# Moving the residual's normalization and the copies of the attention heads in the queues of VectorE and ScalarE

## The reference

```python
x = layer_norm(ALPHA * x + mixer, ln1_g, ln1_b)
q = (x @ wq); k, v = split(mem @ wkv)            # 4 heads of 256, 256 memory tokens
p = softmax(q k^T / 16); o = p v                 # per head
x = layer_norm(ALPHA * x + o @ wo, ln2_g, ln2_b)
```

## Time and profile before

| What | Value |
|---|---|
| Median of 3 runs | 884.2 us (882.92 to 884.68) |
| Profiled execution: its own time | 888.07 us |
| Its span in the trace | 886.3 us |
| Mean granted clock of TensorE | 0.975 |
| PE busy | 856.4 us (97%) |
| PE, DVE and ACT in the chain of work that ended last | 67%, 18% and 8% of the span |
| DVE busy | 666.4 us (75%) |
| ACT busy | 484.6 us (55%) |
| DMA, mean over the span | 188 GB/s |

### The profile page before, as it was taken

The page is one execution under the profiler, slowest core; times in us unless marked ns, Lnnn a source line. Parts: engine busy times, 40 slices in busy tenths (PEclk is TensorE's granted clock), DMA queues, the critical chain, the costliest instruction groups (busy, mean ns, idle before and its releaser), DMA issues.

```text
span 886.3 us, 15964 instructions
## 1 busy us (share of the span) xinstructions
PE 856.4 (97%) x6420; PEld 810.8 (91%) x6420; DVE 666.4 (75%) x1076; ACT 484.6 (55%) x730; POOL 7.7 (1%) x17
## 2 busy tenths in 40 slices
PE   8999999999979999999997999999999999999997
PEld 7889987999879999999997999899899999999885
DVE  5787787867667888888867896787797687776553
ACT  5643456556547666655456756565657454444452
POOL 0200000000000000000000000000000000000000
PEclk9999999999978999999998999999999899999999
DMA  9886658854132766567872365475566377775751
GB/s 338 242 264 197 206 188 245 248 169 133 61 118 85 227 186 181 182 199 262 276 245 85 119 180 157 142 229 171 171 214 190 97 230 227 235 222 183 173 207 48
DMA packets 139593, 166.91 MB, mean 188 GB/s; under 512 B 5520, under 2 KB 123280, under 8 KB 139520
## 3 DMA queue, kind: packets, MB, share of 16 engines
q1 hardware_dynamic: 137712, 162.82, 58.6%
q0 software_dynamic: 720, 2.02, 1.2%
q10 hardware_dynamic: 1088, 1.05, 0.3%
HBM read 164.62 MB, written 1.25 MB: 187 GB/s over the span
## 4 chain that ended last, share of the span: by engine, by line
PE 67%; DVE 18%; ACT 8%; issue 4%; DMA 2%; SPq 1%; DVEq 0%; ACTq 0%
PE ps L529 67%; DVE lor L1721 7%; DVE FA L1724 3%; ACT hir L1161 3%; DVE FA L1721 2%; DMA raw<-in_w_in 1%; DVE raw L1738 1%; DVE X L1721 1%; DVE FA L1727 1%; DMA raw<-in_ffn_w_down 1%; DVE X L1724 0%; DVE FA L2472 0%; ACT FA L1287 0%; ACT FA L1601 0%; PE ps L774 0%
## 5 line engine op out<-in xcount | busy, mean ns | idle before, releaser
L1721 DVE TENSOR_TENSOR lor<-raw,hir 128x1024 fp32r<-128x1024 f32 (+1 forms) x267 | 308.5, 1176 | 93.0 <-ACT hir L1161 90.0
L1161 ACT ACTIVATE hir<-raw 128x1024 fp32r<-128x1024 f32 (+1 forms) x257 | 258.3, 1030 | 103.6 <-PE ps L529 85.1
L529 PE MATMUL ps<-INH,hir 128*128 128x256 f32 (+2 forms) x1000 | 288.7, 289 | 1.8 <-ACT INH L1329 1.2
L529 PE MATMUL ps<-INH,lor 128*128 128x256 f32 (+2 forms) x1000 | 284.6, 285 | 2.8 <-DVE lor L1721 2.7
L529 PE MATMUL ps<-INL,hir 128*128 128x256 f32 (+2 forms) x1000 | 284.9, 285 | 0.8 <-DVE INL L1721 0.6
L529 PE MATMUL ps<-HIH,hir 128*128 128x256 f32 (+1 forms) x752 | 216.6, 288 | 0.0
L529 PE MATMUL ps<-HIH,lor 128*128 128x256 f32 (+1 forms) x752 | 213.6, 284 | 2.1 <-DVE lor L1721 2.1
L529 PE MATMUL ps<-HIL,hir 128*128 128x256 f32 (+1 forms) x752 | 212.5, 283 | 0.0
L529 PEld LDWEIGHTS ps<-INH,lor 128*128 128x128 f32 x1000 | 191.9, 192 | 5.1 <-DVE lor L1721 4.0
L529 PEld LDWEIGHTS ps<-INH,hir 128*128 128x128 f32 x1000 | 192.1, 192 | 4.7 <-issue 3.4
L529 PEld LDWEIGHTS ps<-INL,hir 128*128 128x128 f32 x1000 | 191.8, 192 | 1.7 <-DVE INL L1721 1.7
(11 more groups left out here) (284 smaller groups left out, 802.1 us busy)
## 6 DMA issues: line engine op xcount, KB each, us to landing
raw<-in_w_in SPq DMA_DIRECT2D x64, 512.0 KB, 4.5
raw<-in_mod_wT SPq DMA_DIRECT2D x48, 512.0 KB, 4.7
raw<-in_ffn_w_up SPq DMA_DIRECT2D x44, 512.0 KB, 4.0
raw<-in_w_ffn_in SPq DMA_DIRECT2D x44, 512.0 KB, 4.8
raw<-in_w_ffn_out SPq DMA_DIRECT2D x22, 512.0 KB, 4.7
raw<-in_ffn_w_down SPq DMA_DIRECT2D x20, 512.0 KB, 5.9
raw<-in_xa_wkv SPq DMA_DIRECT2D x16, 512.0 KB, 4.5
raw<-in_xa_wq SPq DMA_DIRECT2D x8, 512.0 KB, 5.1
```

Source lines behind the costliest of these rows:

```text
L529: return e.matmul(o, l, r, start=start, stop=stop, skip_group_check=True)
L1161: e.activation(hi, src, ACT.Copy).then_inc(*w_hi.up(i))
L1721: return e.tensor_tensor(o, a, b, op)
```

## The change

The normalization of the residual is moved in both queues, and the order of the last two heads against the splits. Nothing is added to or taken from what is computed. PE's and SP's own orders are unchanged.

On DVE `normed(0)` goes in front of `settle(0)` and `normed(1)` behind `settle(1)`. `normed(2)` and `normed(3)` stand right behind `shares(3)`, and `next(xo[1])` goes behind all copies and splits of heads 2 and 3. On ACT `affine(0)` stands before `settle(0)`, `affine(1)` before `expo(0)`, and `turned(2)` and `turned(3)` follow `expo(3)` directly; `next(xo[1])` stands behind `oc_put(3)`.

```diff
@@ scalar @@
             ahead.more()
             ahead.more()
-            settle(0)
-            settle(1)
...
+            affine(0)
+            settle(0)
+            settle(1)
             ahead.unit(("xq", 2), 8)
+            affine(1)
             expo(0)
             expo(1)
             settle(2)
...
             oc_put(0)
             oc_put(1)
             expo(3)
-            affine(0)
-            affine(1)
-            next(xo[1])
             turned(2)
             turned(3)
             affine(2)
             oc_put(2)
+            affine(3)
             oc_put(3)
+            next(xo[1])
             next(xo[2])
-            affine(3)
             for c in range(4):
@@ vector @@
             run(late)
+            normed(0)
             settle(0)
             settle(1)
+            normed(1)
             ahead.more()
             ahead.more()
...
             greatest(3)
             oc_put(1)
             shares(3)
-            normed(0)
-            normed(1)
-            next(xo[1])
             normed(2)
+            normed(3)
             oc_copy(2)
             oc_put(2)
             oc_copy(3)
             oc_put(3)
+            next(xo[1])
             next(xo[2])
-            normed(3)
             for c in range(4):
```

## The result

The changed kernel takes 881.86 us (median of 20 runs, 879.02 to 886.11) against 884.55 us for the kernel before, measured beside it (20 runs, 882.92 to 887.68). The ratio is 0.9972 with a 95% interval of 0.9960 to 0.9983, so it is faster by 0.28%, some 2.5 us (the medians differ by 2.7). One execution of the last kernel of the experiments took 1661.23 us, nearly twice as long as any other; it is left out of that kernel's median.

A forecast was written before the change was run, and what follows sets the result against it. PE, busy 97% of the span, was taken as the bound except in a few waits. Terms 0 + 1.1 - 1.05 - 3.1 = -3.05 us gave 881.15 us from a median of 884.2; range 878.6 to 884.6.

The forecast's parts named there:

- a half clock between 221 and 250: Sign that the prediction is wrong: PE's clock at half somewhere from 221 to 250 us, in the memory attention.
- `normed(0)` in DVE's idle time, cost 0: Before 197.80 us DVE idles 1.83 us for PE; normed(0), 1.37 us, fits into it and costs nothing.
- `normed(1)` reaches PE in full, 1.1 us: DVE has no idle time before the splits at 201.60; the delay makes PE begin near 223.0, 1.1 us late.
- Given back out of the wait for ACT's copy: PE's wait of 1.33 us before 231.25 absorbs the lateness, giving back 1.05 us, net loss 0.05.
- 3.6 us the most: PE's floor: residual 0 can't come before 240.5, so at most 3.6 us without changing the pattern.
- The tail, 3.1 us: DVE and ACT from 226 lose two normed and two affine; residual of chunk 0 at 241.0 instead of 244.07.
- Nothing late at 240.5 for the moved split: Second half of xo1 is split by 238.8, PE wants it at 240.5: 1.7 us to spare.
- Rival 2: PE's pause at 221.6 grows to about 1.35 us and its clock falls, losing 4.2 us: 885.3; chance 0.10.
- return "one step later": After a clock fall in the pause at 221.6, full clock returns a step later, making 886.5 instead of 885.3.
- two terms of 0.8 us for friction and for the clock's steps: Allowances in the bounds: 0.8 us of queue friction against the gain, about 0.8 for what clock steps add or take.
- Rival 1: Half-clock stretch still runs 254.7 to 271.8 though work comes earlier, giving back 1.5 us: 882.7; chance 0.20.
- Rival 3: PE's clock stays full through the second normalization, saving 4.5 us more: 876.6; chance 0.07.

The follow-up runs named there:

- last kernel of the experiments: The order only kernel with residual 3 and its square moved in front of the two splits; 878.45 us against 884.73 before, ratio 0.9922.
- chunk 1 late: Changed kernel with normed(1) and affine(1) put back behind the last softmax; 880.80 us against 884.71 before, ratio 0.9957.
- order only: Changed kernel with all four norms behind the last softmax, copies of heads 2 and 3 still ahead of the splits; 880.09 us against 884.71 before, ratio 0.9948.
- norms-only kernel: Changed kernel with norms of chunks 0 and 1 still early, splits and last norm back between and behind the copies; 885.47 us against 884.71 before, ratio 1.0009.
- delay-twice kernel: Changed kernel with two more norm-sized DVE instructions behind normed(1), output unchanged; 883.65 us against 884.73 before, ratio 0.9995.

## Why the prediction was right

Forecast were 881.15 us and a gain of 3.05 us; measured were 881.86 us and a ratio of 0.9972, 2.5 us. The mechanism is the forecast one, but one of the prediction's own signs of being wrong, a half clock between 221 and 250, came in the first trace. Point by point:

- *`normed(0)` in DVE's idle time, cost 0*: right. The idle time shrank from 1.83 to 0.43 us and the scores began where they had (204.62, with the whole stage 0.17 later).
- *`normed(1)` reaches PE in full, 1.1 us*: right and shown both ways. Taken back it gave 1.0 us of B (27.38 to 26.38), doubled it lengthened the pause by another 1.33.
- *Given back out of the wait for ACT's copy*: right for this kernel, from 1.33 to 0.25 us in every trace with the new order. But the wait goes as well where PE is not late (chunk 1 late, order only), so the lateness bought nothing: it is 1.0 us that the change could have kept. The prediction called 3.6 us the most that was to be had, because it took PE's lateness into its floor; the order-only kernel gained 4.0 us in B.
- *The tail, 3.1 us*: right. From head 3's product to three splits in a row to residual 0; B is 2.99 us shorter where the clock did not fall. What carries it is the order, not the early norms: the early norms alone changed nothing that the runs can tell, the order alone gained 4 us. Which part of the order carries it was not tried: in every kernel `normed(3)` moved ahead of the copies together with `next(xo[1])` behind them. The prediction had counted "two `normed` and two `affine`" less as what the tail loses, and that was not the reason. They have cover there: behind the other two norms DVE is idle for head 2 for 3.5 us, 4.48 in the trace with the fall.
- *Nothing late at 240.5 for the moved split*: right. No wait of PE for `lor` near there in any trace.
- *Rival 2, the clock falls in the pause at 221.6*: its mechanism is real and was priced too high. The pause was 1.27 us, below the 1.4 named as the point of decision, and the clock fell in one trace of three of this kernel, in the one of the norms-only kernel (1.26 us), and behind the pause of 2.60 us; behind 0.25 us in none of six. It stayed at half for some 3.4 us and cost 0.94 us, not 4.2 and a return after 5.4 us of work. The prediction's 886.5 for a return "one step later" has no row behind it, nor have its two terms of 0.8 us for friction and for the clock's steps. A third of 0.94 us, taken off 3.0, gives 2.7, near the measured 2.5 and 2.0; this is an estimate, since only three traces of that kernel show the fall or its absence. Of the 0.7 us between forecast and measured time, half is the smaller gain and half the median of before, 884.55 for the 884.2 that the forecast started from.
- *Rival 1, the return at a fixed time*: no. Work came 1.87 us earlier (the first feed-forward product at 263.70 instead of 265.57) and the clock was full again from about 268.8 instead of 271.8, as the windows show (0.80 over the two microseconds, that is 1.2 us at full). In all eleven traces it came back 5.1 to 6.3 us behind the first feed-forward product, wherever that lay:

```profile
266.00:268.00 2.00, 2.00 (x11) 2.00 (x11) 1.83 (x4) 1.97 (x5) 0.00 (x0) 0.50 0.00 0
268.00:270.00 2.00, 2.00 (x16) 2.00 (x16) 1.84 (x3) 1.97 (x5) 0.00 (x0) 0.80 0.00 0
```

- *Rival 3, the clock holds through the normalization*: not in the changed kernel, nor in any other trace. It held into the late sums in the delay-twice kernel, in one of two traces of the order-only kernel, and where residual 3 came without a pause; in the first two C is shorter by 1.1 and 1.4 us for it.
- *The traces differ by 5.1 us*: 1.88 to residual 0 (with A 0.17 longer), 3.2 in D. The second trace of before has a D of 617.8, 0.3 above the changed kernel's, so these 3.2 need not be a part of the change.

The Trainium skill (TensorE: Matmul & The Clock Gate, "What's actually happening") says that the monitor runs freely. By that rule the same pause can cost the clock in one execution and not in the next; the three traces of the changed kernel agree, with the same 1.27 us and one fall.

## What to carry to other kernels

Before moving work to an earlier idle time, look whether it already stands under a wait: here the tail had room for all four norms under a wait for PE, and moving one of them forward cost 1 us that PE saw and put the clock at risk. What cost in these two engines that feed each other was less the work than the number of turns: a piece on DVE that ACT must answer before its next split cost 1.4 us of work and 2.2 of waiting. Put such pieces where both engines wait for a third, keep what only fills buffers behind what the third engine waits for, and cut traces in parts before comparing two of them.

## What the runs showed of the hardware

The same program, with the same pause of 1.27 us in front of the same products, lost PE's full clock in one trace of three, for 3.4 us. Short falls of this kind also lie at places that the change doesn't touch (near 13, 54, 121, 431, 450 to 456 and 617 to 623 us), each in some traces only. The part of the kernel behind this stage varies from 617.4 to 621.3 us between the traces, by up to 2.9 us between two of one kernel. A difference of less than about 3 us between two single traces does not show a difference between kernels here, whereas the stretch B repeats to 0.02 us in the three kernels traced more than once, wherever no fall lies in it. C does not always: the order-only kernel had 21.50 and 20.07.
